# Query and key chunks projected before the gates, keys turned through DRAM, and rotary tables moved, in a two-layer hybrid attention trunk

## What is computed

```python
def hybrid_layer(x, ...):
    h = rms_norm(x, pre_w, NORM_EPS)
    dq, dk, dv, dg, sq, sk, sv, sg, iq, ik, iw = jnp.split(h @ w_in, SPLIT_OFFSETS, axis=-1)
    dq, dk = apply_rope(dq, ...), apply_rope(dk, ...)          # 4 heads x 2 maps x 64
    oa = diff_attention(dq, dk, dv, lam)                       # softmax(map 0) - lam * softmax(map 1)
    oa = rms_norm(oa, subln_w, SUBLN_EPS) * (1.0 - lambda_init) * jax.nn.silu(dg)
    sq, sk, iq = apply_rope(sq, ...), apply_rope(sk, ...), apply_rope(iq, ...)
    ik = apply_rope(layer_norm(ik, ikn_w, ikn_b, LN_EPS), ...)
    ob = dsa_attention(sq, sk, sv, iq, ik, iw)                 # each query attends its 64 best keys by the index scores
    ob = ob * jax.nn.silu(sg)
    return x + rms_norm(concat([oa, ob]) @ w_out, post_w, NORM_EPS)
```

## Time and profile before

| | |
|---|---|
| three timed runs | 303.89, 304.04, 304.04 us; median 304.04 |
| profiled execution | 303.62 us, of which its trace spans 301.8 |
| TensorE busy | 295.1 us, 98% of the span |
| VectorE busy | 235.2 us, 78% |
| ScalarE busy | 164.1 us, 54% |
| GpSimd busy | 69.2 us, 23% |
| DMA | 56.87 MB, mean 188 GB/s, its engines 58% busy |
| granted TensorE clock | 0.997 of full |

### The profile page before, as it was taken

How to read it: one execution, slowest core, us unless ns; L and a number is a source line. 1 busy time by engine, 2 the same in 40 slices (tenths; PEclk the granted TensorE clock), 3 DMA queues, 4 the chain that set the end, 5 groups by cost and what they waited for, 6 DMA issues and landing times.

```text
span 301.8 us, 4431 instructions
## 1 busy us (share of the span) xinstructions
PE 295.1 (98%) x1592; PEld 249.6 (83%) x1592; DVE 235.2 (78%) x476; ACT 164.1 (54%) x284; POOL 69.2 (23%) x116
## 2 busy tenths in 40 slices
PE   8999999999999999999999999999999999999992
PEld 8799777788787888888888988778878788888892
DVE  4753989799999987973984786878999999778333
ACT  5886853645677464503665855473737747370101
POOL 6558500303031120001070740011303031110101
PEclk9999999999999999999999999999999999999998
DMA  7999959457519578221059799947653775300011
GB/s 252 367 370 386 368 210 365 139 125 241 201 43 233 185 247 311 64 59 38 0 156 369 246 348 246 294 144 197 208 151 129 140 279 156 125 2 0 0 72 70
DMA packets 49110, 56.87 MB, mean 188 GB/s; under 512 B 21952, under 2 KB 26816, under 8 KB 49088
## 3 DMA queue, kind: packets, MB, share of 16 engines
q1 hardware_dynamic: 48800, 56.33, 57.7%
q10 hardware_dynamic: 288, 0.26, 0.3%
HBM read 52.91 MB, written 3.67 MB: 187 GB/s over the span
## 4 chain that ended last, share of the span: by engine, by line
PE 98%; DVE 0%; POOLq 0%; issue 0%; DVEq 0%; ACT 0%; POOL 0%; ACTq 0%
PE bank_a L437 20%; PE bank_a L446 20%; PE bank_a L442 20%; PE bank_a L595 7%; PE bank_s L595 6%; PE bank_t L416 4%; PE bank_a L454 4%; PE bank_o L572 4%; PE bank_s L555 2%; PE bank_s L535 1%; PE bank_s L547 1%; PE bank_o L724 1%; PE bank_t L595 1%; PE bank_o L446 1%; PE bank_s L446 1%; PE bank_o L442 1%
## 5 line engine op out<-in xcount | busy, mean ns | idle before, releaser
L965 DVE TENSOR_TENSOR w_lo<-w_raw,w_hi 128x2048 fp32r<-128x2048 f32 (+1 forms) x46 | 98.4, 2149 | 18.0 <-ACT w_hi L741 17.7
L741 ACT ACTIVATE w_hi<-w_raw 128x2048 fp32r<-128x2048 f32 (+1 forms) x46 | 81.9, 1784 | 32.3 <-PE bank_a L446 24.0
L437 PE MATMUL bank_a<-w_hi,h_hi 128*128 128x512 f32 (+1 forms) x272 | 72.7, 389 | 0.0
L446 PE MATMUL bank_a<-w_lo,h_hi 128*128 128x512 f32 (+1 forms) x272 | 70.1, 379 | 0.0
L442 PE MATMUL bank_a<-w_hi,h_lo 128*128 128x512 f32 (+1 forms) x272 | 70.0, 379 | 0.0
L446 PEld LDWEIGHTS bank_a<-w_lo,h_hi 128*128 128x128 f32 x272 | 49.6, 188 | 10.3 <-DVE w_lo L965 0.8
L442 PEld LDWEIGHTS bank_a<-w_hi,h_lo 128*128 128x128 f32 x272 | 49.8, 188 | 9.8
L437 PEld LDWEIGHTS bank_a<-w_hi,h_hi 128*128 128x128 f32 x272 | 47.8, 188 | 10.3 <-issue 2.7
L809 ACT ACTIVATE xt_pbuf<-xt_pbuf,st 128x128 f32<-128x128 f32 (+1 forms) x48 | 21.2, 444 | 24.0 <-DVE st L1097 24.0
L1391 POOL TENSOR_TENSOR rt<-nat,tab 128x256 f32<-128x256 f32 x10 | 7.4, 742 | 112.2 <-ACT nat L793 112.1
L793 ACT ACTIVATE nat<-bank_a,st 128x512 f32<-128x512 f32 x20 | 13.5, 681 | 19.6 <-PE bank_a L446 19.6
(11 more groups left out here) (194 smaller groups left out, 444.9 us busy)
## 6 DMA issues: line engine op xcount, KB each, us to landing
w_raw<-in_w_in SPq DMA_DIRECT2D x30, 1024.0 KB, 6.0
w_raw<-in_w_out SPq DMA_DIRECT2D x8, 1024.0 KB, 6.1
w_raw<-in_w_in SPq DMA_DIRECT2D x8, 584.0 KB, 7.5
turned<-mixn SPq DMA_DIRECT2D x20, 128.0 KB, 2.7
prm<-in_rows SPq DMA_DIRECT2D x2, 705.0 KB, 7.0
w_raw<-in_w_in SPq DMA_DIRECT2D x2, 512.0 KB, 6.4
xres<-in_x SPq DMA_DIRECT2D x2, 512.0 KB, 9.6
dqT<-turned SPq DMA_DIRECT2D x2, 512.0 KB, 5.8
```

The costliest lines, as they stand in the source:

```text
L437: pe.matmul(bank, h_hi[:, HALF * half + kk, tok], whi[:, kk, :], start=half == 0 and kk == 0, stop=False)
L446: mm = pe.matmul(bank, h_hi[:, HALF * half + kk, tok], wlo[:, kk, :], start=False, stop=half == 1 and kk == HALF - 1)
L741: act.activation(unit(w_hi, u), unit(raw, u), ACT.Copy).then_inc(hi_done.sem, 1)
L965: dve.tensor_tensor(unit(w_lo, u), unit(raw, u), unit(w_hi, u).bitcast(F32), ALU.subtract).then_inc(lo_done.sem, 1)
```

## The change

The chunk order becomes IQ, MIXED, DQ, DK, DG, SG, SQ, SK, DV, SV: the third and fourth chunk, groups 4 to 7 and units 4 to 7, are now the differential query and key, and DG's narrow units are 8 and 9. dk is turned as dq is: VectorE squares, a fourth DRAM scratch tensor, `dk_squares`, `dk_put`, `dk_landed`, and two reads in place of one. `turn_nat(T_DK)` and its two drains go, so later T uses are numbered two lower. SyncE, TensorE, ScalarE and VectorE get new orders to match; the index key's statistics split off from `index_key` and come earlier. On GpSimd the first rotary table is built ahead of `root_x(0, 0)`, the second behind `rope(DK)` of layer 0. The core of the diff:

```diff
-IQ, MIXED, DG, SG, DQ, DK, SQ, SK, DV, SV = range(10)
-PARTS = (8, 9, 3, 7, 0, 1, 4, 5, 2, 6)
+IQ, MIXED, DQ, DK, DG, SG, SQ, SK, DV, SV = range(10)
...
-T_IK, T_DK, T_PD0, T_PD1A, T_SK, T_PD1B = 4, 5, 7, 8, 9, 11
...
+T_IK, T_PD0, T_PD1A, T_SK, T_PD1B = 4, 5, 6, 7, 9
...
                 for u in range(UNITS - RING):
-                    if layer and u == 8:
+                    if layer and u == 7:
                         sp.wait_ge(iq_squares, 1)
                         put(0, iq_put)
-                    if layer and u == 9:
+                    if layer and u == 8:
                         sp.wait_ge(iq_put, 16 * SQUARES)
                         get(0, iqT, iq_landed)
-                    if u == 13:
+                    if u == 8:
                         sp.wait_ge(dq_squares.sem, dq_squares.at(layer, 1))
                         put(1, dq_put.sem)
-                    if u == 14:
+                    if u == 9:
                         sp.wait_ge(dq_put.sem, dq_put.at(layer, 16 * SQUARES))
                         get(1, dqT, dq_landed.sem)
+                    if u == 11:
+                        sp.wait_ge(dk_squares.sem, dk_squares.at(layer, 1))
+                        put(2, dk_put.sem)
+                    if u == 12:
+                        sp.wait_ge(dk_put.sem, dk_put.at(layer, 16 * SQUARES))
+                        for b in range(BLOCKS):
+                            sp.dma_start(dkT[:, :, b * P:(b + 1) * P], scratch[2][:, b * HEADS:(b + 1) * HEADS, :]).then_inc(dk_landed.sem, 16)
                     if u == 16:
                         sp.wait_ge(sq_squares.sem, sq_squares.at(layer, 1))
-                        put(2, sq_put.sem)
+                        put(3, sq_put.sem)
...
+                pe.wait_ge(ik_ready.sem, ik_ready.at(layer, 1))
+                turn(T_IK, [ik2[:, b, :, :].rearrange("p t d -> p (t d)") for b in range(BLOCKS)])
                 first(7)
                 second(7)
-                pe.wait_ge(ik_ready.sem, ik_ready.at(layer, 1))
-                turn(T_IK, [ik2[:, b, :, :].rearrange("p t d -> p (t d)") for b in range(BLOCKS)])
-                first(8)
...
+                pe.wait_ge(proj_moved.sem, proj_moved.at(layer, 6))
                 index_logits(0, 0, range(4))
                 index_logits(2, 1, (0, 1))
+                first(8)
                 second(8)
-                first(9)
                 index_logits(4, 1, (2, 3))
-                second(9)
-                first(10)
-                second(10)
-                first(11)
-                second(11)
+                for g in range(9, 12):
+                    first(g)
+                    second(g)
                 first(12)
                 second(12)
-                turn_nat(T_DK, 0, 3)
                 first(13)
...
-                pe.wait_ge(t_drained.sem, t_drained.at(layer, T_DK + 2))
-                pe.wait_ge(dq_landed.sem, dq_landed.at(layer, dq_landed.per_layer))
+                pe.wait_ge(dq_landed.sem, dq_landed.at(layer, 16))
+                pe.wait_ge(dk_landed.sem, dk_landed.at(layer, 16 * BLOCKS))
...
                 second(14)
                 first(15)
+                diff_scores(10, 1, (2, 3))
+                second(15)
                 pe.wait_ge(combined.sem, combined.at(layer, 1))
                 turn_probs(T_PD0, 6, 0, HEADS)
-                diff_scores(10, 1, (2, 3))
-                second(15)
+                first(16)
+                second(16)
                 pe.wait_ge(combined.sem, combined.at(layer, 2))
                 turn_probs(T_PD1A, 8, 1, 2)
-                first(16)
-                second(16)
                 turn_nat(T_SK, 0, 5)
                 first(17)
@@ -671,7 +678,7 @@
                 turn_probs(T_PD1B, 10, 1, 2)
...
+                    if chunk == DK:
+                        if layer:
+                            act.wait_ge(iq_squares, 1)
+                        else:
+                            act.wait_ge(iq_filled, 2)
                     if chunk == SQ:
                         act.wait_ge(dq_squares.sem, dq_squares.at(layer, 1))
+                    if chunk == SK:
+                        act.wait_ge(dk_squares.sem, dk_squares.at(layer, 1))
...
-                for g in range(4, 8):
+                for g in range(4, 7):
                     move(g)
                     split_hi(layer, g + 4)
-                relu(0)
-                relu(1)
+                move(7)
+                for j in range(4):
+                    relu(j)
+                split_hi(layer, 11)
                 move(8)
-                relu(2)
-                relu(3)
-                split_hi(layer, 12)
                 relu(4)
                 relu(5)
+                split_hi(layer, 12)
                 move(9)
...
                 split_hi(layer, 16)
+                move(13)
                 exps(6, 0, 4)
                 exps(7, 0, 4)
-                move(13)
                 split_hi(layer, 17)
                 exps(8, 1, 2)
                 exps(9, 1, 2)
                 move(14)
                 split_hi(layer, 18)
+                move(15)
                 exps(10, 1, 2)
                 exps(11, 1, 2)
-                move(15)
...
-                def index_key():
...
                     ins.then_inc(ik_var.sem, 1)
+                def index_key():
...
                     drain_x(layer, 1)
                 split_lo(layer, 4)
                 split_lo(layer, 5)
-                split_lo(layer, 6)
+                key_stats()
...
-                split_lo(layer, 7)
+                split_lo(layer, 6)
                 if layer:
                     turn_squares(0, 1, iq_squares)
-                split_lo(layer, 8)
+                split_lo(layer, 7)
                 index_key()
+                if layer:
+                    dve.wait_ge(iq_put, 16 * SQUARES)
+                turn_squares(1, 2, dq_squares.sem)
...
+                drain(T_IK, ikT[:, :])
+                split_lo(layer, 8)
                 split_lo(layer, 9)
-                drain(T_IK, ikT[:, :])
                 split_lo(layer, 10)
-                split_lo(layer, 11)
...
                 index_sum(0, 0, (0, 2, 4, 6))
                 index_sum(1, 0, (1, 3, 5, 7))
+                dve.wait_ge(dq_put.sem, dq_put.at(layer, 16 * SQUARES))
+                turn_squares(0, 3, dk_squares.sem)
...
                 index_sum(2, 1, (0, 2))
                 index_sum(3, 1, (1, 3))
-                split_lo(layer, 12)
+                split_lo(layer, 11)
                 index_sum(4, 1, (4, 6))
                 index_sum(5, 1, (5, 7))
-                if layer:
-                    dve.wait_ge(iq_put, 16 * SQUARES)
-                turn_squares(1, 2, dq_squares.sem)
                 choose(0, 4)
-                split_lo(layer, 13)
+                split_lo(layer, 12)
                 choose(0, 4)
...
+                split_lo(layer, 13)
                 split_lo(layer, 14)
-                choose(1, 1)
-                drain_pair(T_DK, dkT)
-                choose(1, 2)
                 split_lo(layer, 15)
+                choose(1, 4)
                 mask_scores(6, 0, 4, causal[:, P:SEQ])
                 mask_scores(7, 0, 4, causal[:, P:SEQ])
-                choose(1, 2)
+                mask_scores(8, 1, 2, causal[:, :])
+                mask_scores(9, 1, 2, causal[:, :])
...
+                split_lo(layer, 16)
+                choose(1, 1)
+                dve.wait_ge(dk_put.sem, dk_put.at(layer, 16 * SQUARES))
+                turn_squares(1, 4, sq_squares.sem)
                 combine(6, 0, HEADS, 0)
-                mask_scores(8, 1, 2, causal[:, :])
-                mask_scores(9, 1, 2, causal[:, :])
-                dve.wait_ge(dq_put.sem, dq_put.at(layer, 16 * SQUARES))
-                turn_squares(1, 4, sq_squares.sem)
-                split_lo(layer, 16)
-                combine(8, 1, 2, 0)
-                drain(T_PD0, pT[:, 0, :])
+                split_lo(layer, 17)
                 mask_scores(10, 1, 2, causal[:, :])
                 mask_scores(11, 1, 2, causal[:, :])
-                split_lo(layer, 17)
-                choose(1, 2)
+                drain(T_PD0, pT[:, 0, :])
+                combine(8, 1, 2, 0)
+                combine(10, 1, 2, 2)
                 drain(T_PD1A, pT[:, 1, :])
-                combine(10, 1, 2, 2)
-                choose(1, 1)
-                mask_unchosen(1)
                 drain_pair(T_SK, skT)
                 split_lo(layer, 18)
                 drain(T_PD1B, pT[:, 2, :])
                 mask_scores(12, 0, 4, work[0][:, :])
+                choose(1, 3)
+                mask_unchosen(1)
                 split_lo(layer, 19)
                 split_lo(layer, 20)
...
-            def rotary_tables():
...
-                for t, heads, half, at in ((0, IDX_HEADS, HD, 0), (2, HEADS, HS, HD)):
+                for t, heads, half, at in tables:
...
                 if layer:
                     root_x(layer, 1)
-                else:
```

(24 more changed lines are left out.)

12 lines of the change are left out of this document (8 added, 4 removed).

## The result

The changed kernel takes 307.16 us (median; 306.64 to 307.26) and the kernel before 303.97 on the same chip: a ratio of 1.0101 (95% interval 1.0085 to 1.0117), 1.0% slower. The forecast was 303.4 with a range of 302.1 to 305.1. The profiled executions took 307.14 and 303.62, with spans of 305.3 and 301.8 and granted clocks of 0.995 and 0.997, so the loss of 3.5 is in waits and not in the clock.

A forecast was written before the change was run, and what follows sets the result against it. TensorE was taken to bound the kernel, with 98% of the chain. The terms -1.77 - 0.61 + 0.62 - 0.10 + 1.22 = -0.64 gave 302.98 profiled and 303.4 for the median, range 302.1 to 305.1.

The forecast's parts named there:

- dk's transposes go: TensorE ahead of first(13): eight transposes cost 0.88 us a layer, so removing them gives -1.77 over two layers.
- old waits of units 6 and 7 go: Layer 0 opening: TensorE's two stalls for low halves of units 6 and 7 disappear, -0.61 us.
- units 4 and 5 wide: Layer 0, chunk 2: TensorE waits for unit 4's low half, not unit 5's, +0.62 us; bounds nothing and 1.4.
- iq and index key adjacent: Layer 0 on TensorE: index transposes and the index key's become neighbours, saving one slow restart, -0.10 us.
- second use of T_SK: TensorE waits for the bank T_PD1A just filled: 0.71 less 0.10 saved restart, 0.61 a layer, +1.22 us.
- gates late: VectorE's gates at T_MD1 and T_MS0: the sum counted no wait of TensorE; lateness appeared only as a rival.
- rival 3: choose(1, 3) and mask make gate_diff(1) late; from 1.4 on each microsecond costs one a layer: 304.6 to 307.0, chance 0.20.
- The bank wait: Wait between T_SK's two uses until VectorE's copy frees the T bank, 0.71 us; bounds 0.3 to 1.2 a layer.
- the rotary tables: GpSimd: first table fits 5.38 us of idle time ahead of root_x, second goes behind rope(DK); costs nothing.
- dk's landing: dk's way through DRAM: squares near 52, dkT near 64, wanted near 75 after first(13); covered, costs nothing.
- the index scores: Layer 1: iq's way through DRAM unchanged, reader about 1.6 us later, nothing; waits for index logits' inputs would show error.
- low 11 and low 13: VectorE's new order: low 11 three and low 13 one microsecond ahead of the TensorE group that reads it.

The follow-up runs named there:

- The run without the wait: Changed kernel with sk's transposes ahead of first(17) and those of block 1's probabilities behind it: 305.89 us, 1.0052 to the kernel before.
- the runs without that wait: Changed kernel with masks 13 and 14 ahead of low 21: 303.78 us; or with two passes of choose(1, 3) ahead of mask_scores(10): 303.62 us.

## Why the prediction was wrong

By its own steps, in us of the profiled execution, both layers. The measured ones are distances between starts; for dk's transposes those of the run that has them back:

| step | forecast | measured |
|---|---|---|
| dk's transposes go | -1.77 | -1.79 |
| old waits of units 6 and 7 go | -0.61 | -0.61 |
| units 4 and 5 wide | +0.62 | +1.34 |
| chunk 2 starts later | none | +0.32 |
| iq and index key adjacent | -0.10 | -0.03 |
| second use of T_SK | +1.22 | +1.16 |
| gates late | 0 (rival 3: 1.2 to 3.6) | +3.16 |
| sum | -0.64 | +3.55, where the starts give 3.52 |

- **The gates: the step that failed.** The sum put this term at nothing. Rival 3 had the mechanism and the place, with a chance of 0.20, a lateness of 0.6 and a margin of 1.40. Both sizes were wrong. The lateness of gate_diff(1) was 1.76 (its end moved from 122.43 to 124.86, by 2.43, and TensorE by 0.67). I had read GpSimd's first root as 1 us long and hadn't asked what runs beside it when the lows move; I named a GpSimd step that stretches only for T_SK. In the kernel before VectorE idled 1.20 ahead of gate_diff(0), and the later lows could have used that up; with the power at 2.97 it still idles 0.94, so that much of the lateness goes back to the root. The other 0.82 is near the 0.6 of the forecast. And I took the margin of one gate. gate_dsa(0) ended at 128.52 for TensorE's 128.79, a margin of 0.27, and nothing between the two gates on VectorE has slack: copy, low 22, drain, copy, gate, back to back. So the formula "from 1.4 on, each microsecond costs one" had its threshold more than a microsecond too high (0.27 and not 1.40): for 1.76 it gives 0.36 a layer, 0.7 in all, and the starts show 1.6 in layer 0. T_MD1 began 0.41 later against the group ahead of it, the products behind it took 0.26 more, since they wait for the copy of `pT` behind the gate, and T_MS0 cost 0.92. Layer 1 has 1.56.
- **Units 4 and 5: mechanism right, size wrong.** The stated bound of 1.4 is nearly reached in this profile (1.34) and passed in others (1.03 to 1.95 over 10.88 in the ten traces with x ahead of the units). The interval of 2.71 was that of units 6 and 7, between whose landings little more than one unit's bytes can move (1.06 MB at 390 GB/s); units 4 and 5 had the x of the residual ahead of them, and with x behind them they too came 2.71 apart. It was also wrong that the high halves are in time: high 5 ended at 26.65 and TensorE was there at 26.37.
- **Chunk 2's start** was in no term. It lies between 22.8 and 23.5 in the traces of all the kernels, though none of them edits anything before it but the tables' place, x's and the parameters', and goes with first tiles that land some tenths earlier or later (in the changed kernel's profile ScalarE starts the second tile at 6.20 and not 5.70, and TensorE waits 0.52 for it); I count it as chance.
- **The bank wait: mechanism right, the net price by some luck.** The forecast was a wait of 0.71 less a saved restart of 0.10. The run without the wait puts the wait at 0.60, and against the kernel before it saves only 0.02 (27.40 for 27.42 from the differential scores to the DSA scores, layer 0), so two misses of about 0.1 cancel. The idle time in the list reads 0.35 and the distances 0.58, so the list alone would have priced it too low.
- **The transposes, the rotary tables, dk's landing, the index scores, low 11 and low 13: right.** dk's squares start at 53.49 (52 in the forecast) and none of these makes TensorE wait.

Without the gates the sum would be +0.39 and the median near 304.4, within the range; the runs without that wait took 303.78 and 303.62. The chances were too kind for a change that reorders VectorE, with the tighter of the two gates' margins unread.

## What to carry to other kernels

Where a change reorders an engine that is off the critical path, list every point at which the bound engine takes something from it, with the margin of each, and price the change at the smallest margin of a run of work that has no slack inside. When work moves, ask of each small GpSimd step what VectorE runs beside it in the new place (here 2.97 us beside a low and 1.01 outside). Where the DMA engines never paused, the interval of two units went from 3.56 us to 2.71 when 1 MB moved from ahead of them to behind: take the interval from a stretch with the same loads ahead, and send what nobody needs soon behind what is needed first.

## What the runs showed of the hardware

- A power of 128x4 numbers on GpSimd took 2.97 us when it started inside a VectorE subtraction of two SBUF operands (128x2048), 1.01 to 1.05 outside; it ended 0.91 after the subtraction. The index key's power, 128x2, took 2.62 beside low 7, and 0.72 in the kernel before, where it started behind the last low.
- Eight transposes of 128x128 in float32 cost TensorE 0.89 us with the slow restart of the next group (1.01 for 0.91), though their records of 0.27 add to 2.2.
- With the DMA engines busy without a pause at 387 to 406 GB/s (15 to 27 us of the changed kernel and of the run with x behind unit 5), a unit of 1 MB landed 2.71 us behind its forerunner where x's 1 MB was issued behind both, and 3.3 to 4.2 in ten traces where x was issued ahead of both; programs with the same opening varied by 0.9 from trace to trace.
